# The merge gates of the first layer by high and low parts of their weights, half a unit at a time

## The reference, cut to what matters

```python
proj = h @ w_in
u, v, gate_b, rec_b, q, kv, nsa_g, xd, mg = jnp.split(proj, cuts, axis=-1)
...
branch = jnp.einsum('nbsc,ncd->bsnd', ys, w_branch)
gates = jax.nn.sigmoid(mg.reshape(B, S, N_BRANCH, D_MODEL))
merged = jnp.sum(gates * branch, axis=2)
return merged @ w_out
```

## Time and profile before

| what | value |
|---|---|
| median of 3 runs | 1901.58 us (1901.45 to 1905.17) |
| the profiled execution | 1908.11 us, its span 1906.3 us |
| TensorE busy | 1851.7 us, 97% of the span |
| VectorE busy | 1137.2 us, 60% |
| ScalarE busy | 856.3 us, 45% |
| GpSimd busy | 44.2 us, 2% |
| bytes moved | 363.53 MB, mean 191 GB/s |
| mean granted TensorE clock | 0.986 |

### The profile page before, as it was taken

One profiled execution on the slowest core, in us unless ns is written; L12 is line 12 of the kernel. 1 busy time (PEld: TensorE's weight loads), 2 busy tenths in 40 slices (PEclk: granted clock), 3 DMA queues, 4 the chain that ended last, 5 costly groups with the idle time before them and its releaser, 6 DMA issues.

```text
span 1906.3 us, 25204 instructions
## 1 busy us (share of the span) xinstructions
PE 1851.7 (97%) x10560; PEld 1574.5 (83%) x10560; DVE 1137.2 (60%) x1415; ACT 856.3 (45%) x1059; POOL 44.2 (2%) x107
## 2 busy tenths in 40 slices
PE   8999999999999999999999999999999989999998
PEld 7998788878888887788788898888788879787886
DVE  5315435479898898544468956545654456746453
ACT  4413321367677675444323245444444345535442
POOL 0030000000000000000000000000000000000000
PEclk9989999999999999999999999999999989999999
DMA  9342334479998887545333007554555434226540
GB/s 362 131 155 89 111 111 155 184 273 360 338 350 342 341 341 303 193 183 199 132 119 125 25 1 291 194 179 178 209 185 186 168 133 155 89 89 254 186 179 33
DMA packets 51232, 363.53 MB, mean 191 GB/s; under 512 B 5681, under 2 KB 5809, under 8 KB 8497
## 3 DMA queue, kind: packets, MB, share of 16 engines
q1 hardware_dynamic: 50976, 359.83, 50.8%
q10 hardware_dynamic: 144, 2.10, 0.3%
HBM read 360.86 MB, written 1.05 MB: 190 GB/s over the span
## 4 chain that ended last, share of the span: by engine, by line
PE 89%; DVE 6%; ACT 3%; issue 1%; POOL 0%; DMA 0%; SPq 0%; POOLq 0%; DVEq 0%; ACTq 0%
PE bank L2139 10%; PE bank L2546 8%; PE bank L2548 8%; PE bank L2547 8%; PE bank L2573 4%; PE bank L2571 4%; PE bank L2572 4%; PE bank L2085 4%; PE bank L2438 3%; PE bank L2440 3%; PE bank L2124 3%; PE bank L2439 3%; PE bank L2269 3%; PE bank L2361 3%; PE bank L2453 2%; PE bank L2455 2%
## 5 line engine op out<-in xcount | busy, mean ns | idle before, releaser
L1249 DVE TENSOR_TENSOR w_a<-ring,w_a 128x2048 fp32r<-128x2048 f32 x221 | 504.3, 2290 | 280.9 <-ACT w_a L779 280.5
L779 ACT ACTIVATE w_a<-ring 128x2048 fp32r<-128x2048 f32 x221 | 420.3, 1912 | 188.2 <-PE bank L2573 90.1
L2546 PE MATMUL bank<-w_a,h 128*128 128x512 f32 x536 | 213.2, 398 | 6.0 <-DVE h L1304 6.0
L2548 PE MATMUL bank<-w_a,h 128*128 128x512 f32 x536 | 209.9, 392 | 0.0
L2547 PE MATMUL bank<-w_a,h 128*128 128x512 f32 x536 | 209.4, 391 | 0.0
L1249 DVE TENSOR_TENSOR w_b<-ring,w_b 128x2048 fp32r<-128x2048 f32 x62 | 142.0, 2291 | 67.8 <-ACT w_b L779 67.1
L2139 PE MATMUL bank<-H,ring 128*128 128x256 f32 x800 | 181.6, 385 | 0.0
L2139 PEld LDWEIGHTS bank<-H,ring 128*128 128x128 f32 x800 | 151.7, 192 | 22.8 <-issue 2.6
L779 ACT ACTIVATE w_b<-ring 128x2048 fp32r<-128x2048 f32 x62 | 118.7, 1914 | 45.7 <-PE bank L2573 25.8
L2546 PEld LDWEIGHTS bank<-w_a,h 128*128 128x128 f32 x536 | 101.1, 189 | 27.3 <-DVE h L1304 4.8
L1021 ACT ACTIVATE sil<-bank,tiny 128x256 f32<-128x256 f32 x88 | 41.7, 474 | 176.5 <-PE bank L2548 176.5
(11 more groups left out here) (466 smaller groups left out, 3155.6 us busy)
## 6 DMA issues: line engine op xcount, KB each, us to landing
ring<-in_stream SPq DMA_DIRECT2D x330, 1024.0 KB, 4.9
G<-in_gains SPq DMA_DIRECT2D x15, 512.0 KB, 5.7
arena<-in_cmp_w ACTq DMA_DIRECT2D x1, 2048.0 KB, 8.1
sm<-in_small SPq DMA_DIRECT2D x1, 1582.0 KB, 13.1
con<-in_consts SPq DMA_DIRECT2D x1, 1032.0 KB, 17.0
X<-in_x SPq DMA_DIRECT2D x2, 512.0 KB, 4.9
out_x<-X SPq DMA_DIRECT2D x2, 512.0 KB, 2.6
sm<-in_small SPq DMA_DIRECT2D x1, 730.5 KB, 23.1
```

Source lines behind the costliest of these rows:

```text
L779: act.activation(w_slot(unit)[:, 0, :], ring[:, unit % RING, :], ACT.Copy).then_inc(S("w_hi"), 1)
L1249: dve.tensor_tensor(w_slot(unit)[:, 1, :], ring[:, unit % RING, :], w_slot(unit)[:, 0, :].bitcast(FP32), ALU.subtract).then_inc(S("w_lo"), 1)
L2546: pe.matmul(bank[4 + t][:, :], x_hi, w[0][:, k, :], start=first, stop=False)
L2548: ins = pe.matmul(bank[4 + t][:, :], x_lo, w[0][:, k, :], start=False, stop=end)
```

## The change

- Each half of an `mg` unit is split like the earlier units, into `gate_w`: two places of 128 x 2048, one for first halves and one for second halves, each with a high part (128 x 1024) and a low part. They lie in the first place of the split weights.
- `gate_split(m)` is a new function on ACT (the high part) and on DVE (the low part). The first two halves are split before the list. Half m + 2 is split at the end of the item that uses half m, after that item's side work and slot. The place is free when TensorE has used half m (`gate_used` for a first half, `unit_used` for a second).
- TensorE's `half_unit` waits for the low part (`gate_lo`) and does `halves` with `h_hi` and `h_lo` in place of `project` with `H`.
- A ring place of an `mg` unit is released by the split of its second half, no longer by its use.
- `h_hi` and `h_lo` have to live through the gates. So the gates get two buffers of eight tiles (`gates_a`, `gates_b`) for two branches at a time in place of 32 tiles, and the compression weights with the recurrence's buffers (`cmp_area`) move onto `G` and `H`. The gain of the norm after the mixer is loaded late: at the last unit of `w_out`, when `y_b` is done.
- The Gelu at item 3 on ACT moves to item 5, behind that item's gate.

```diff
+MG_ITEMS = [i for i, (kind, n, part) in enumerate(ITEMS) if kind == "mg"]
...
+        with nc.sbuf_tensor("cmp_area", [P, 2 * 32 * HD], FP32) as cmp_area:
+            pass
         G = sb("G", [P, 2, D])
...
+        gate_w = [[w_a[:, 0, part, a * KD * P:(a + 1) * KD * P].rearrange("p (k n) -> p k n", k=KD) for a in range(2)] for part in range(2)]
+        cut(2 * UNIT)
         yc = tiles(cut(MT * T), MT)
         yd = tiles(cut(MT * T), MT)
-        mg = tiles(cut(4 * KD * T), 4 * KD)
-        after_mg = cut.at
-        cw1_flat = cut(2 * 32 * HD)
+        gates_a = tiles(cut(KD * T), KD)
+        cw1_flat = cmp_area[:, :]
...
-        late = arena[:, after_mg - 16 * T:after_mg]
...
+        windows = arena[:, cut.at:cut.at + 2 * MT * (16 + T)]
...
+        gates_b = tiles(cut(KD * T), KD)
+
+        def gates_of(n, d0):
+
+            return (gates_a, gates_b)[BR_ORDER.index(n) % 2 if n in BR_ORDER[:2] else n - 1][:, d0:d0 + 2, :]
...
+        for m, i in enumerate(MG_ITEMS):
+            RELEASE[FULL[f"mg{ITEMS[i][1]}"][1] - 1] = ("gate_lo", m + 1)
...
-        def schedule(run_slot, run_item):
+        def gate_half(m):
+
+            _, n, part = ITEMS[MG_ITEMS[m]]
+            unit = FULL[f"mg{n}"][1] - 1
+            return unit, ring[:, unit % RING, :].rearrange("p (k n) -> p k n", k=KD)[:, :, part * P:(part + 1) * P], gate_w[part]
+
+        def schedule(run_slot, run_item, gate_split=lambda m: None):
 
             for i in range(len(ITEMS)):
                 run_item(i)
                 if i >= SLOT_FROM and i - SLOT_FROM < N_SLOTS + 3:
                     run_slot(i - SLOT_FROM)
+                if i in MG_ITEMS and MG_ITEMS.index(i) + 2 < len(MG_ITEMS):
+                    gate_split(MG_ITEMS.index(i) + 2)
...
-                ("moe", "proj"), ("ffn0", "moe"), ("ab", "ffn0"), ("ffn1", "ab"), ("ffn2", "ffn1"), ("c", "ffn2"),
+                ("ffn0", "moe"), ("ab", "ffn0"), ("ffn1", "ab"), ("ffn2", "ffn1"), ("c", "ffn2"),
...
+                if u == D_UNITS["w_out"] + SQUARE - 1:
+                    sp.wait_ge(S("y_b"), 1)
+                    load_gain(NB["moe"], 1)
...
+            def gate_split(m):
+
+                unit, src, dst = gate_half(m)
+                act.wait_ge(S(f"unit{unit % RING}"), 16 * (unit // RING + 1))
+                if m < 2:
+                    act.wait_ge(S("unit_used"), FULL["vw"][1])
+                elif m % 2 == 0:
+                    act.wait_ge(S("gate_used"), m // 2)
+                else:
+                    act.wait_ge(S("unit_used"), gate_half(m - 2)[0] + 1)
+                act.activation(dst[0], src, ACT.Copy).then_inc(S("gate_hi"), 1)
+
...
             evac("g24", gates3[:, :, :], ACT.Tanh, scale=0.5)
+            for m in range(2):
+                gate_split(m)
...
-                    evac(f"mg{n}", mg[:, 2 * n:2 * n + 2, :], ACT.Tanh, scale=0.5)
-                if i == 3:
+                    if n // 4 == BR_ORDER[3] + 1:
+                        act.wait_ge(S("br_added"), 4)
+                    evac(f"mg{n}", gates_of(n // 4, 2 * (n % 4)), ACT.Tanh, scale=0.5)
+                if i == 5:
                     act.wait_ge(S("side_full"), SI["hid"] + 1)
...
-            schedule(run_slot, run_item)
+            schedule(run_slot, run_item, gate_split)
...
+            def gate_split(m):
+
+                unit, src, dst = gate_half(m)
+                dve.wait_ge(S("gate_hi"), m + 1)
+                dve.tensor_tensor(dst[1], src, dst[0].bitcast(FP32), ALU.subtract).then_inc(S("gate_lo"), 1)
+
+            for m in range(2):
+                gate_split(m)
...
-                    link(dve.tensor_tensor(SQ[:, d0:d0 + 2, :], SQ[:, d0:d0 + 2, :], gates, ALU.add))
+                    dve.tensor_tensor(SQ[:, d0:d0 + 2, :], SQ[:, d0:d0 + 2, :], gates, ALU.add).then_inc(S("br_added"), 1)
+                    dve.wait_ge(S("br_added"), 4 * (BR_ORDER.index(n // 2) - 1) + 2 * (n % 2) + part + 1)
...
-            schedule(run_slot, run_item)
+            schedule(run_slot, run_item, gate_split)
...
-            def half_unit(name, half):
-
-                n = FULL[name][1] - 1
-                if half == 0:
-                    unit_channels(group_begin(name), unit_ready(n), (0,))
-                else:
-                    unit_channels(bank[5 + GI[name] % 2], ring[:, n % RING, :].rearrange("p (k n) -> p k n", k=KD), (1,))
+            def half_unit(m):
+
+                _, n, part = ITEMS[MG_ITEMS[m]]
+                ps = group_begin(f"mg{n}") if part == 0 else bank[5 + GI[f"mg{n}"] % 2]
+                pe.wait_ge(S("gate_lo"), m + 1)
+                halves(ps[:, part * T:(part + 1) * T], lambda a, k: gate_w[part][a][:, k, :], h_hi, h_lo, KD)\
+                    .then_inc(S("unit_used" if part else "gate_used"), 1)
```

More of the change, by code:

```diff
@@ L357, in build @@
         p_cmp = tiles(cut(4 * P), 2)
-        late = arena[:, after_mg - 16 * T:after_mg]
-        win_a, win_b = (tiles(late[:, n * MT * (16 + T):(n + 1) * MT * (16 + T)], MT) for n in range(2))
         hid_c = cut(2 * 16).rearrange("p (c n) -> p c n", c=2)
@@ L363, in build @@
         first_cols = tiles(cut(4 * 16), 4)
+        windows = arena[:, cut.at:cut.at + 2 * MT * (16 + T)]
+        win_a, win_b = (tiles(windows[:, n * MT * (16 + T):(n + 1) * MT * (16 + T)], MT) for n in range(2))
+        gates_b = tiles(cut(KD * T), KD)
+        def gates_of(n, d0):
+            return (gates_a, gates_b)[BR_ORDER.index(n) % 2 if n in BR_ORDER[:2] else n - 1][:, d0:d0 + 2, :]
+        assert cut.at <= SPLIT_AREA - 2 * KD * T
         assert cut.at <= SPLIT_AREA
@@ L1484, in branch_out @@
                 d0 = 4 * (n % 2) + 2 * part
-                of, last = KD * (n // 2) + d0, n // 2 == BR_ORDER[-1]
+                last = n // 2 == BR_ORDER[-1]
                 dve.wait_ge(S(FULL[name][0]), FULL[name][1])
                 dve.wait_ge(S("proj_free"), GI[name])
-                gates = mg[:, of:of + 2, :]
+                gates = gates_of(n // 2, d0)
                 dst = SQ[:, d0:d0 + 2, :] if n // 2 == BR_ORDER[0] else gates
@@ L2289, in run_item @@
                 if kind == "mg":
-                    half_unit(f"mg{n}", part)
+                    half_unit(MG_ITEMS.index(i))
                 else:
```

## The result

| | before | after |
|---|---|---|
| median | 1903.38 us (4 runs, 1901.45 to 1906.14) | 1913.5 us (4 runs, 1911.9 to 1913.8) |
| ratio | | 1.0036, 95% interval 1.0019 to 1.0052 |
| the profiled execution | 1908.11 us, span 1906.3 | 1911.9 us, span 1910.1 |
| mean granted TensorE clock | 0.986 | 0.985 |

The change makes the kernel slower: by 10.1 us (0.53%) on these medians, by 0.36% (0.19 to 0.52%) in the ratio on record. Four runs a side leave the size open within some 4 to 11 us; the last experiment, with more runs, has 6.4 us between its medians. The forecast was 1912.0, with 1903 to 1923 as its range.

The account below looks back on a forecast made before the run. The prediction took TensorE's own work to bound the items before the change. It set 17.9 us saved against 28.3 of waits and clock: +10.4 on a median of 1901.6, so 1912.0 us, range 1903 to 1923.

Parts of the forecast that it names:

- A half unit: Each gate half on TensorE: 2.88 us split against 3.44 plain, saving 0.56, for 32 halves 17.9 us.
- Before `compress_hidden`: Item 5: TensorE idles 3.6 us, as DVE's low part of half 6 is queued ahead of `compress_halves`.
- before `compress_out`: TensorE idles 2.0 us for the Gelu, now behind the unit's Tanh and a table load.
- The clock in items 4 to 6: Half clock to about 148.5: half 4 takes about 5.5 us, half 5 4.5, with some half clock in half 6.
- Items 8 to 11: Plain items, nothing saved; DVE arrives late for the scores of item 8 and item 9's turn: 1.9 us more.
- The slots: Items 12 to 19 and 24 to 32: ACT and DVE chain sets wide slots' pace; 3.5 us saved, bounds 2 and 9.5.
- Item 36: TensorE idles 7.7 us, as DVE's low part of half 28 is queued behind `recur_2` and its reciprocal.
- The clock behind it: Items 36 to 39: half clock for the first stretch after the long gap costs 2.3 us, bounds 0 and 3.
- The first, a clock that recovers at once: Clock recovers at once in items 5, 6 and 36: lag +5.6 us, time 1907; chance 0.2.
- The second, a clock that keeps falling in the slots: Half clock for a third of the 100 us of slots: +13 us more, time 1925; chance 0.12.
- The third, slots that hide their splits: Slot chain shorter than its rows' sum, 6 us of waits gone; lag about 0, time 1901; chance 0.08.
- The fourth: DVE and ACT stay ahead everywhere and TensorE alone sets the end: -17.9 us, time 1883.7; chance 0.05.

Follow-up runs that it names:

- the last experiment: The changed kernel timed and profiled again with no edit, against the kernel before: 1912.32 us, ratio 1.0043.
- the fourth experiment: Changed kernel with ACT's high part ahead of the slot, `recur_2` in quarters, and Gelu and compression work ahead in items 4 and 5: 1892.72 us, ratio 0.9929.
- the third experiment: Changed kernel with the Gelu ahead of the gate's Tanh and splits of halves 6 and 7 behind the compression work: 1910.41 us, ratio 1.0017.
- the eighth: Changed kernel with its moves of buffers and of the Gelu but no gate splits, gates multiplied plain: 1908.2 us, ratio 1.0014.
- the first experiment: Changed kernel with ACT making the high part before the slot's `exp` and `weights_out`, not behind them: 1912.54 us, ratio 1.0028.
- the fifth experiment: Changed kernel with 28 unused products on TensorE in the gap before item 36: 1915.76 us, one run.
- the three edits: On the changed kernel: high part ahead of the slot, `recur_2` in quarters, reordered items 4 and 5; together 1892.72 us, singly 1912.54, 1912.05 and 1910.41.
- the ninth: Kernel with the three edits, but `recur_2` quarters at items 35, 37 and two at 38, square root and `recur_3` at 40: 1892.53 us, ratio 0.9933.

## Why the prediction was right

Counted from the start of item 0, the changed kernel is behind the old one at the prediction's marks by:

| mark | predicted | measured |
|---|---|---|
| item 4 | -1.3 | -0.8 |
| item 8 | +5.3 | +6.3 |
| item 12 | +7.2 | +8.9 |
| item 33 | +3.7 | +4.8 |
| item 36 | +10.0 | +11.0 |
| item 40 | +10.4 | +10.8 |
| `w_out` | +10.4 | +10.7 |

The mechanism was right: the waits stand where the prediction put them, and taking each away by order alone takes its time away; only at items 8 to 11 part of the reason was missing. That the sum came within 0.3 us is in part luck, since terms of up to 1 us were off both ways. That 1912.0 lies so near 1913.5 is luck as well: its base of 1901.6 was the median of three runs, and in the 13 to 29 runs beside the experiments the kernel before has 1905.95 to 1907.3; from there the same sum gives 1916.4 to 1917.7, 3 to 5 us above what was measured and still inside the range.

**A half unit** takes 2.93 us as a row of its own and 2.89 in an unbroken run (17.35 us for six) against 2.88 expected, and 3.32 to 3.43 plain. The gain was there; the fourth experiment gets the stage 12.4 us under the kernel before by order alone.

**Items 0 to 3** won 0.8, not 1.3: the two waits were 0.65 and 0.55 as rows of the timeline have them, against 0.5 and 0.4, and the wait before `compress_halves` was 2.38 for 2.21 before the change.

**Before `compress_hidden`** 3.57 for 3.6, and **before `compress_out`** 2.45 for 2.0. Both by the chain that the prediction named; the third experiment takes both away by changing the order. The Gelu's share is the same with no splits at all in the eighth (2.3 us).

**The clock in items 4 to 6** was mis-sized. Half 5 was put at 4.5, between 2.88 and 5.76, and measured 5.15 (5.20 in the last experiment). With 0.45 more before `compress_out`, and 0.2 less from there to half 7 (5.97 for 6.2), this makes the mark of item 8 come 1.0 later than forecast. What came before cancelled: item 4 began 0.5 late and the narrow products took 13.7, not 12.9, but half 4 took 4.4, not 5.5, so half 4 was done when it should be, counted from item 0.

**Items 8 to 11** cost 2.6, not 1.9. DVE was late for the scores of item 8, as forecast, but not by its own work alone: it had stood still for ACT's high part of half 8, which came behind `exp` of the first slot.

```profile
167.09 1.23 DVE L1376 TENSOR_TENSOR w_a<-ring,w_a 128x1024 fp32r<-128x1024 f32 x1 [1.71 <-ACT w_a L876]
```

With ACT's split ahead of the slot, and all of DVE's work still there, the four items take 19.33 us, as before the change. So the prediction had the place right, and left out of the reason what the order on ACT adds to it.

**The slots** won 4.1 for 3.5, within the bounds. That they are set by the chain of `soft_1`, `exp`, `weights_out`, high part and low part is shown by the first experiment, which cuts that chain in one place and wins another 5.2 between items 12 and 33 (96.34 to 91.15).

**Item 36** waited 7.48 for 7.7, behind the reciprocal of 6.55. Quartering it leaves 1.47 of the wait.

**The clock behind it** cost 1.7 (the fifth experiment), not 2.3, but 2.5 to 2.7 in two other kernels with the same gap.

**The moves** cost nothing but the Gelu's place, as said; the eighth experiment shows it.

**The table load.** It takes 1.28 us, as in the earlier trace rows, and the next activation starts 1.30 us after the load does (157.16 to 158.46). The price of some 2.7 us a switch in the Trainium skill (ScalarE: Activation LUTs, What ACT_TABLE_LOAD costs) isn't seen here. By an estimate from that page's figure, 1.4 us more than the load alone, the gap before `compress_out` would have been near 4; it is 2.45.

**The rivals.** The first, a clock that recovers at once, is excluded by 0.50 at 152 and 160 and by 5.15 us for half 5. The second, a clock that keeps falling in the slots, is excluded: the halves in the slots take about 2.93. The third, slots that hide their splits, is excluded by the gaps in them, by the 4.1 us won of the 9.5 that it needs, and by what cutting the chain wins. The fourth named the right lever: it was to decide at item 34 and at half 6, and both were as the code's order said. With the order changed there and in the slots the stage is 12.4 us shorter than before, of the 17.9 that it named; so the fourth was wrong on this kernel, and on the one beside it right in its direction.

**The sum against the median.** The stage says +10.7, the medians +10.1 at first and +6.4 (1912.32 against 1905.95) in the last experiment, where the intervals of the ratios overlap (1.0019 to 1.0052 and 1.0027 to 1.0058, or 3.6 to 11 us). The profiled executions differ by only 3.8. In these the difference of 9.4 behind `w_out` shrinks to 6.8 at 947 us and to 3.8 from 1142 on, in steps that lie where the granted clock of one or the other is at half for some 3 us: the kernel before has 31 us of half clock between `w_out` and the last product, the changed one 20. Why the clock falls at a place in one execution and not in the next was not found out.

What stays open besides: 0.9 us by which the three edits together win more than one by one in and before items 8 to 11, and why three halves behind the same gap of 7.5 us took 10.39 to 11.41 us.

## What to carry to other kernels

When an engine starts to prepare data for the one that sets the pace, look up its queue and ask for each piece of preparation what stands in front of it and what now stands behind it; sums of busy time (here 60% and 45%) say nothing on that. Cut a long instruction on the preparing engine, such as the reciprocal of 128 x 1024, into pieces shorter than the lead of the buffers, and put the preparation ahead of a slot's work, not behind it: three such changes of order turned 0.4% slower into 0.7% faster. Read the gain of an edit at the marks of its stage, as the total of a long kernel moves by several us with where the clock falls.

## What the runs showed of the hardware

- A busy TensorE doesn't always keep its clock, or get it back. In the experiment with half 4 first it was busy for 100% of 129 to 140 us, the clock at 1.00 up to 137, some 4.5 us into the narrow products of 36 columns, and at 0.50 from there. With the narrow products mixed with full ones of 256 columns, behind a wait of 2.37 us, it was busy for 100% of 130 to 145 us, and its granted clock was 0.50 throughout.
- How long the narrow products take depends on what comes before them: 64 records took 9.67 us behind a half unit of full products with no gap, and 12.0 to 13.7 behind a gap of 2.2 to 2.4 us.
- The time in which the clock is at half behind the stage changes with small shifts of the whole: 41 us between `w_out` and the last product for the first experiment and 24 for the ninth, in the same code. In that first experiment 13.6 us of it at 370 to 384 took a lead of 5.5 us down to 0.6.
- A reciprocal costs more by column than the other wide operations that DVE does in this stage: 6.55 us for 128x1024 and 1.75 for 128x256, where an operation on two such tiles takes 1.22 and 0.42.
